# Two transformer blocks: queries scaled by a negative factor when they leave PSUM, a row minimum as the shift of the softmax, and the low parts of the woven-in weights made in two halves

## The chip, the cores and the metric

The kernel runs on one core of one Trainium2 chip. The metric is the time of one execution on the device, in microseconds; the time before is the median of three runs.

## The reference

Two blocks are computed on a sequence of 512 positions with 1024 features, in float32: the first with two layers, the second with one. What matters here are the four softmax attentions. Cut to that:

```python
scale = MLA_QK ** -0.5                          # mla: 8 heads, all 512 keys
s = (einsum('bqhd,bkhd->bhqk', qn, k_nope) + einsum('bqhr,bkr->bhqk', qr, k_r)) * scale
probs = softmax(s, axis=-1)
...
# gqa: 8 heads of 64, a window of 128 keys to either side, alibi slopes 2 ** (-(h + 1)), a sink logit a head
# dsa: 8 heads of 64, the 128 keys that an index score picks, causal by chunks, scale 64 ** -0.5
# mem: 4 heads of 128 over 256 memory rows, scale 128 ** -0.5
```

Around them stand projections, gates, a Fourier mix, a linear recurrence and gated feed-forward networks, all with weights that come from HBM in float32.

## The kernel before, in words

**Products in three parts.** A float32 product with a weight is made of three matmuls: high part by high part, high by low, low by high (`mac`, L549 to L551 for 512 columns). The weights come in one long stream of units of 16 blocks of 128x128 (2048 columns, 1 MB). Every unit goes the same way: SyncE loads it into `raw`, ScalarE (ACT) copies it to `w_hi`, VectorE (DVE) subtracts to get `w_lo` (`split_unit`, L1504) and signals `lo_ready`, which frees both TensorE (PE) to use it and SyncE to load the next but one unit into the same buffer. There are two buffers of each kind.

**The stages.** A layer of the first block has among others z1 and uq (query and key projections), mla, gqa, am, cm, wout, gu and dn; the second block has z2, dsa, mq, mem, mo and again a feed-forward network. The order on each engine is written out by hand; engines meet at semaphores alone.

**Attention.** `attention` exists once for each engine. An item is one head with one block of 128 queries: 32 items in mla, gqa and dsa, 16 in mem, so 176 in the whole program (mla and gqa run twice). For item t

- PE makes the scores (L679) into one of two banks. In gqa and dsa scores are made in pairs, t even and t + 1, once `shift_ready` says that both items before have their shift; in mla and mem one at a time, once the exponential of item t - 2 is done. Behind that it turns the probabilities of item t - 3 (L701), multiplies values (L726, L737), and then does a few blocks of another stage that is woven in: 2 blocks of z1b an item in mla, 3 of am in gqa, 2 of mk in dsa (and mv), none in mem.
- DVE adds the bias where there is one (L1708), takes the row maximum `st_max` (L1713), multiplies it by -scale to `st_neg` (L1714) and signals `shift_ready`; then, for item t - 1, it takes the reciprocal of the sum (L1723) and multiplies the probabilities by it (L1725). Behind that comes `also(t)`: the evictions of the woven-in stage and its split.
- ACT copies the turned probabilities of item t - 3 out of PSUM (`pT`, L1201), and takes the exponential with `st_neg` as bias and the scale as factor (L1212).

**The woven-in stage.** On DVE it is `after_blocks` (L1682): in item t it evicts what PE finished in item t - 1, and splits a unit whose last block PE did in item t - 2.

```python
for b in beside(st, t - 2, per) if t >= 2 else ():
    if b % BLK == BLK - 1 or b == TILES[st][-1][-1]:
        split_unit(c, st, b // BLK)
```

A unit has 16 blocks. Per layer 2 units end in z1b and 6 in am; in the second block 2 end in mk. That makes 18 splits. The two units of mv are split by a call of their own.

**Queries.** They leave PSUM as they are: in z1 and z1b (`qc`) and z2 (`qd`) by `copy_out` (L1533), in uq (`q_a`) by a copy on ACT and a product with the rotary factors on DVE (L1863), in mq (`mq`) by a product with the norm's factor (L2093).

## Time and profile before

| what | value |
|---|---|
| median of 3 runs | 2875.31 us (2872.71 to 2878.05) |
| the profiled execution | 2874.89 us |
| its span | 2873.0 us |
| PE busy | 2727.7 us, 95% |
| DVE busy | 1452.4 us, 51% |
| ACT busy | 1112.2 us, 39% |
| POOL (GpSimd) busy | 378.7 us, 13% |
| granted clock of TensorE, mean | 0.983 of full speed |
| mla, first and second layer, roughly | 211 to 297 us, 1143 to 1227 us |
| gqa, first and second layer, roughly | 297 to 400 us, 1227 to 1338 us |
| dsa, mem, roughly | 2204 to 2293 us, 2434 to 2463 us |

Times in the trace count from the start of the span. PEld is PE's loading of weights, which overlaps its matmuls; L12 is line 12 of the kernel. A row of the timeline gives start, duration, engine, line, operation, and in brackets how long the engine sat idle before it and what released it. Matmuls overlap in their records, so that the sum of durations says little; the distance of starts is what counts.

### The profile page before, as it was taken

To read this page: it belongs to the slowest core of one execution; us is meant where nothing else is said; L and a number is where in the kernel's file an instruction comes from. 1 tells how busy PE (TensorE), PEld (TensorE's weight loads), DVE (VectorE), ACT (ScalarE), POOL (GpSimd) and SP (SyncE) were. 2 spreads that over 40 slices of the span, in tenths; PEclk is the share of its full clock that TensorE was granted. 3 is DMA by queue.
4 is the path that set the end of the run, shared out by engine and by line. 5 is a ranking of instruction groups with operands and counts; after the bars stand their busy time and mean duration, and the time that the engine had idled before them with its cause. 6 is when DMAs were issued, how large, how long until landed. Compare 5 with 4: busy or idle time off the path is not lost. (4 is left out here: it accounts for less than half of the span.)

```text
span 2873.0 us, 37336 instructions
## 1 busy us (share of the span) xinstructions
PE 2727.7 (95%) x13556; PEld 2193.9 (76%) x13556; DVE 1452.4 (51%) x2215; ACT 1112.2 (39%) x1733; POOL 378.7 (13%) x299
## 2 busy tenths in 40 slices
PE   5999999999999799999999999989898899899998
PEld 4876678988887687667898888767686588788886
DVE  5556654533324655665353332455588636634333
ACT  4345543422224434554342222433633534522221
POOL 1010001311102201000131110320011012311101
PEclk9999999999999899999999999999999999999999
DMA  3321122222232232011322223212232122122222
GB/s 125 128 88 45 33 72 96 81 102 96 94 117 88 69 121 99 30 45 60 106 76 96 102 95 111 88 64 83 74 118 74 59 84 93 40 92 88 102 103 88
DMA packets 37057, 245.96 MB, mean 86 GB/s; under 512 B 4144, under 2 KB 5168, under 8 KB 7984
## 3 DMA queue, kind: packets, MB, share of 16 engines
q1 hardware_dynamic: 33600, 239.09, 23.9%
q10 hardware_dynamic: 3312, 4.93, 0.5%
q8 instruction: 91, 1.49, 0.2%
q14 instruction: 54, 0.44, 0.0%
HBM read 241.91 MB, written 2.10 MB: 85 GB/s over the span
## 5 line engine op out<-in xcount | busy, mean ns | idle before, releaser
L549 PE MATMUL bank<-h_hi,w_hi 128*128 128x512 f32 x2024 | 806.4, 398 | 12.1 <-POOL h_lo L2110 4.7
L551 PE MATMUL bank<-h_hi,w_lo 128*128 128x512 f32 x2024 | 791.1, 391 | 0.0
L550 PE MATMUL bank<-h_lo,w_hi 128*128 128x512 f32 x2024 | 791.0, 391 | 0.0
L1504 DVE TENSOR_TENSOR w_lo<-raw,w_hi 128x2048 fp32r<-128x2048 f32 x153 | 353.4, 2310 | 367.1 <-ACT w_hi L1048 365.7
L549 PEld LDWEIGHTS bank<-h_hi,w_hi 128*128 128x128 f32 x2024 | 381.6, 189 | 105.7 <-issue 19.0
L551 PEld LDWEIGHTS bank<-h_hi,w_lo 128*128 128x128 f32 x2024 | 381.4, 188 | 80.8
L550 PEld LDWEIGHTS bank<-h_lo,w_hi 128*128 128x128 f32 x2024 | 381.9, 189 | 79.7 <-issue 3.4
L1048 ACT ACTIVATE w_hi<-raw 128x2048 fp32r<-128x2048 f32 x153 | 291.9, 1910 | 224.1 <-PE bank L551 217.5
L1516 DVE TENSOR_TENSOR w_lo<-raw,w_hi 128x2048 fp32r<-128x2048 f32 x62 | 142.0, 2292 | 158.0 <-ACT w_hi L1260 156.5
L550 PE MATMUL bank<-a_lo,w_hi 128*128 128x512 f32 x528 | 205.4, 389 | 0.0
L549 PE MATMUL bank<-a_hi,w_hi 128*128 128x512 f32 x528 | 205.4, 389 | 0.0
L551 PE MATMUL bank<-a_hi,w_lo 128*128 128x512 f32 x528 | 205.4, 389 | 0.0
L2128 POOL TENSOR_TENSOR a_lo<-res,a_hi 128x512 f32 x66 | 91.3, 1386 | 619.4 <-ACT a_hi L1256 564.1
L1765 DVE TENSOR_TENSOR res<-bank,rstd 128x512 f32<-128x512 f32 x60 | 41.5, 691 | 235.0 <-PE bank L551 235.0
L1256 ACT ACTIVATE a_hi<-res 128x512 f32 x60 | 37.9, 632 | 293.6 <-DVE res L1768 293.6
L1201 ACT ACTIVATE pT<-bank 128x512 f32<-128x512 f32 (+3 forms) x168 | 82.9, 493 | 113.7 <-PE bank L701 112.1
L2110 POOL TENSOR_TENSOR m_lo<-res,m_hi 128x512 fp32r<-128x512 f32 x24 | 31.1, 1294 | 697.0 <-ACT m_hi L1097 697.0
L549 PEld LDWEIGHTS bank<-a_hi,w_hi 128*128 128x128 f32 x528 | 99.1, 188 | 20.8
L551 PEld LDWEIGHTS bank<-a_hi,w_lo 128*128 128x128 f32 x528 | 99.1, 188 | 20.6
L550 PEld LDWEIGHTS bank<-a_lo,w_hi 128*128 128x128 f32 x528 | 99.1, 188 | 20.4
L1260 ACT ACTIVATE w_hi<-raw 128x2048 fp32r<-128x2048 f32 x60 | 114.1, 1902 | 0.0
L1254 ACT ACTIVATE sg<-sg 128x512 f32<-128x512 f32 x60 | 38.0, 633 | 177.3 <-DVE sg L1762 177.3
(397 smaller groups left out, 4401.0 us busy)
## 6 DMA issues: line engine op xcount, KB each, us to landing
raw<-in_stream SPq DMA_DIRECT2D x226, 1024.0 KB, 4.8
x<-in_xT SPq DMA_DIRECT2D x2, 1024.0 KB, 12.6
out_T<-x ACTq DMA_DIRECT2D x8, 256.0 KB, 2.1
p_f<-in_pT ACTq DMA_DIRECT2D x2, 512.0 KB, 3.9
memf<-in_memT ACTq DMA_DIRECT2D x1, 1024.0 KB, 5.6
cst_sb<-in_cst ACTq DMA_DIRECT2D x1, 411.5 KB, 6.5
pos_i<-in_pos ACTq DMA_DIRECT2D x1, 258.0 KB, 9.1
vec<-in_vec ACTq DMA_DIRECT2D x2, 26.0 KB, 1.7
```

The source lines that it names most:

```text
L549: nc.tensor.matmul(ps, wh, xh, start=start, stop=False)
L550: nc.tensor.matmul(ps, wh, xl, start=False, stop=False)
L551: return nc.tensor.matmul(ps, wl, xh, start=False, stop=stop)
L1048: nc.scalar.activation(home(c, v)[0][:, :], raw[v % 2][:, :], ACT.Copy).then_inc(hi_ready, 1)
L1201: nc.scalar.activation(a["pT"][h % 2][:, 0:n, b * P:(b + 1) * P], TURNED[:, 0:n * P].rearrange("p (t q) -> p t q", t=n), ACT.Copy).then_in ...
L1254: nc.scalar.activation(sg[:, p, :], sg[:, p, :], ACT.Silu).then_inc(act_took, 1)
L1256: nc.scalar.activation(a_hi[:, bass.ds(i * 2 + p, 1), :].rearrange("p a s -> p (a s)"), res[:, p, :], ACT.Copy).then_inc(res_hi, 1)
L1260: nc.scalar.activation(w_hi[v][:, :], raw[v][:, :], ACT.Copy).then_inc(hi_ready, 1)
L1504: nc.vector.tensor_tensor(lo[:, :], raw[v % 2][:, :], hi[:, :].bitcast(F32), ALU.subtract).then_inc(lo_ready, 1)
L1516: nc.vector.tensor_tensor(w_lo[s][:, :], raw[s][:, :], w_hi[s][:, :].bitcast(F32), ALU.subtract).then_inc(lo_ready, 1)
L1765: nc.vector.tensor_tensor(res[:, p, :], bank[(t0 + 2 * p + 1) % 4][:, :], rstd[:, 0, :], ALU.mult).then_inc(tile_free, 1)
L2128: nc.gpsimd.tensor_tensor(a_lo[:, bass.ds(i * 2 + p, 1), :].rearrange("p a s -> p (a s)"), res[:, p, :], a_hi[:, bass.ds(i * 2 + p, 1), :] ...
```

## The change

All four attentions now hold negated, scaled logits in PSUM. The queries are multiplied by -scale on their way out of PSUM (`scale_out` in z1, z1b and z2; a factor on ACT and in a three-operand product in uq and mq). The bias gets the opposite sign and loses its factor, the sink as well. The row minimum of that is the shift as it stands, so DVE writes it straight to `st_neg`, and `st_max` and the multiply behind it are gone. The exponential has the factor -1.

The splits of the woven-in stages are cut in two pieces of 1024 columns. The first is made where the whole was made, the second one item later, and the second one signals `lo_ready`. `also` is called once more behind the last item, for the second piece of the last unit. The splits of all other stages, the two of mv among them, stay whole.

```diff
--- before.py
+++ after.py
@@ -260,7 +260,6 @@
         sq = sb("sq", 108, [2, S])
         rstd = sb("rstd", 112, [2, S])
         sq_acc = rstd[:, 1, :]
-        st_max = sb("st_max", 116, [32])
         st_neg = sb("st_neg", 116.25, [32])
         st_sum = sb("st_sum", 116.5, [32])
         st_rec = sb("st_rec", 116.75, [32])
@@ -1185,7 +1184,7 @@
 
                 def set_sink(t):
                     nc.scalar.activation(a["prob"][t % 4][:, 0:1], vv("sink", items[t][0]), ACT.Copy,
-                                         scale=1 / a["scale"]).then_inc(sink_set, 1)
+                                         scale=-1.0).then_inc(sink_set, 1)
                 for t in range(4) if sink else ():
                     set_sink(t)
                 for t in range(len(items) + LAG):
@@ -1210,7 +1209,7 @@
                         n += a.get("first", 0)
                         src = a["prob"][t % 4] if a["biased"] else SCORES[t % 2]
                         nc.scalar.activation(a["prob"][t % 4][:, 0:n], src[:, 0:n], ACT.Exp, bias=st_neg[:, t:t + 1],
-                                             scale=a["scale"], accum_out=st_sum[:, t:t + 1]).then_inc(exp_done, 1)
+                                             scale=-1.0, accum_out=st_sum[:, t:t + 1]).then_inc(exp_done, 1)
                         if sink and t + 4 < len(items):
                             act.wait_ge(exp_done, c.at("I", st, t + 1))
                             set_sink(t + 4)
@@ -1320,7 +1319,7 @@
 
                 def evac_uq(n):
                     if n < 8:
-                        take_hi(c, "uq", n, n, q_a[0:NOPE, n, :], src=lambda ps: ps[0:NOPE, :])
+                        take_hi(c, "uq", n, n, q_a[0:NOPE, n, :], src=lambda ps: ps[0:NOPE, :], scale=-ATT["mla"]["scale"])
                     elif n < 12:
                         j = 2 * (n - 8)
                         take_hi(c, "uq", n, n, k_a[j // 4][0:NOPE, j % 4, :], src=lambda ps: ps[0:NOPE, :])
@@ -1531,6 +1530,10 @@
                 else:
                     dve.wait_ge(tile_done, c.at("T", st, n + 1))
                 nc.vector.tensor_copy(dst, src(ps_of(c, st, n))).then_inc(tile_free, 1)
+
+            def scale_out(c, st, n, dst, factor):
+                dve.wait_ge(tile_done, c.at("T", st, n + 1))
+                nc.vector.tensor_scalar(dst, ps_of(c, st, n)[:, :], factor, None, ALU.mult).then_inc(tile_free, 1)
 
             def pass_on(c, st, n):
 
@@ -1685,9 +1688,19 @@
                     for n, tile in enumerate(TILES[st]):
                         if tile[-1] == b:
                             evac(n)
-                for b in beside(st, t - 2, per) if t >= 2 else ():
-                    if b % BLK == BLK - 1 or b == TILES[st][-1][-1]:
-                        split_unit(c, st, b // BLK)
+                for piece in range(2):
+                    for b in beside(st, t - 2 - piece, per) if t >= 2 + piece else ():
+                        if b % BLK == BLK - 1 or b == TILES[st][-1][-1]:
+                            split_piece(c, st, b // BLK, piece)
+
+            def split_piece(c, st, u, piece):
+
+                v = c.base[st]["U"] + u + 2
+                dve.wait_ge(hi_ready, c.at("U", st, u + 3))
+                at = slice(piece * UC // 2, (piece + 1) * UC // 2)
+                ins = nc.vector.tensor_tensor(w_lo[v % 2][:, at], raw[v % 2][:, at], w_hi[v % 2][:, at].bitcast(F32), ALU.subtract)
+                if piece == 1:
+                    ins.then_inc(lo_ready, 1)
 
             def attention(c, st, bias=None, sink=False, also=None):
                 a = ATT[st]
@@ -1710,8 +1723,7 @@
                             n += lo
                         if sink:
                             dve.wait_ge(sink_set, c.layer * len(items) + (t + 1))
-                        link(nc.vector.reduce_max(st_max[:, t:t + 1], src[:, 0:n], AX_X))
-                        nc.vector.tensor_scalar(st_neg[:, t:t + 1], st_max[:, t:t + 1], -a["scale"], None, ALU.mult).then_inc(shift_ready, 1)
+                        nc.vector.tensor_reduce(st_neg[:, t:t + 1], src[:, 0:n], AX_X, ALU.min).then_inc(shift_ready, 1)
                     if a["per_tile"] == 2 and t % 8 == 3 and 11 <= t < len(items):
                         output_lo(c, st, taken)
                         taken += 1
@@ -1728,6 +1740,8 @@
                             taken += 1
                     if also is not None:
                         also(t)
+                if also is not None:
+                    also(len(items) + 2)
                 while taken < a["heads"] // a["per_tile"]:
                     output_lo(c, st, taken)
                     taken += 1
@@ -1854,13 +1868,14 @@
                             nc.vector.scalar_tensor_tensor(out=dst, in0=cq[:, j, :], scalar=vv("q_norm", j) if j < 3 else vv("kv_norm"),
                                                            in1=rstd[:, j // 3, :], op0=ALU.mult, op1=ALU.mult).then_inc(res_ready, 1)
                     else:
-                        copy_out(c, "z1", n, n, qc[:, n - 6, :], lambda ps: ps[:, :], wait_act=False)
+                        scale_out(c, "z1", n, qc[:, n - 6, :], -ATT["gqa"]["scale"])
                 stage_loop(c, "z1", evac_z1)
 
                 def evac_uq(n):
                     if n < 8:
                         dve.wait_ge(act_took, c.at("A", "uq", n + 1))
-                        nc.vector.tensor_tensor(q_a[64:P, n, :], ps_of(c, "uq", n)[64:P, :], cs[64:P, :], ALU.mult).then_inc(tile_free, 1)
+                        nc.vector.scalar_tensor_tensor(out=q_a[64:P, n, :], in0=ps_of(c, "uq", n)[64:P, :], scalar=-ATT["mla"]["scale"],
+                                                       in1=cs[64:P, :], op0=ALU.mult, op1=ALU.mult).then_inc(tile_free, 1)
                     elif n < 12:
                         j = 2 * (n - 8) + 1
                         copy_out(c, "uq", n, n, k_a[j // 4][0:NOPE, j % 4, :], lambda ps: ps[64:P, :])
@@ -1874,7 +1889,7 @@
                     link(nc.vector.tensor_tensor(dist[:, b, 0:n], dist[:, b, 0:n], cst_sb[:, CST["window"] + off:CST["window"] + off + n], ALU.add))
                 def evac_z1b(n):
                     if n < 2:
-                        copy_out(c, "z1b", n, 0, qc[:, 2 + n, :], lambda ps: ps[:, :], wait_act=False)
+                        scale_out(c, "z1b", n, qc[:, 2 + n, :], -ATT["gqa"]["scale"])
                     else:
                         dve.wait_ge(act_took, c.at("A", "z1b", 1))
                         pass_on(c, "z1b", 2)
@@ -1883,7 +1898,7 @@
 
                 def alibi(h, b):
 
-                    return dist[:, b, 0:len(windowed(b)) * P], -(2.0 ** (-8.0 * (h + 1) / HEADS)) * HD ** 0.5
+                    return dist[:, b, 0:len(windowed(b)) * P], 2.0 ** (-8.0 * (h + 1) / HEADS)
                 def add_am(n):
 
                     if n % 2 == 1:
@@ -2020,7 +2035,10 @@
                         link(nc.vector.tensor_scalar(wsc[:, :, :], vw[:, :, HD:HD + 8], 8 ** -0.5, None, ALU.mult))
                 else:
                     dst = {8: ki, 22: kk}.get(n)
-                    copy_out(c, "z2", n, 0, qd[:, n - 18, :] if dst is None else dst[:, :], lambda ps: ps[:, :], wait_act=False)
+                    if dst is None:
+                        scale_out(c, "z2", n, qd[:, n - 18, :], -ATT["dsa"]["scale"])
+                    else:
+                        copy_out(c, "z2", n, 0, dst[:, :], lambda ps: ps[:, :], wait_act=False)
                 for t in idx_items(n):
                     add_idx(t)
                 if n >= 18:
@@ -2082,7 +2100,7 @@
                     left("mv", (t - 28) // 4, (t - 28) // 4)
                 if t in (25, 33):
                     split_unit(c, "mv", (t - 25) // 8)
-            attention(c, "dsa", lambda h, b: (score[:, b, 0:(b + 1) * P], 1.0), also=evac_mem)
+            attention(c, "dsa", lambda h, b: (score[:, b, 0:(b + 1) * P], -1.0), also=evac_mem)
             merge(c, 2, "cm", 2)
             project_norm(c, "wout", "post1", 2, "mix_post", "normh")
             for half in range(2):
@@ -2090,8 +2108,9 @@
                 for p in range(2):
                     dve.wait_ge(tile_done, c.at("T", "mq", 2 * half + p + 1))
                     for g in range(2):
-                        ins = nc.vector.tensor_tensor(mq[:, 2 * p + g, cols(half)], ps_of(c, "mq", 2 * half + p)[:, cols(g)],
-                                                      rstd[:, 0, cols(half)], ALU.mult)
+                        ins = nc.vector.scalar_tensor_tensor(out=mq[:, 2 * p + g, cols(half)], in0=ps_of(c, "mq", 2 * half + p)[:, cols(g)],
+                                                             scalar=-ATT["mem"]["scale"], in1=rstd[:, 0, cols(half)],
+                                                             op0=ALU.mult, op1=ALU.mult)
                     ins.then_inc(tile_free, 1)
                 if half == 0:
                     for u in range(2):
```

**Where instructions move.** Both places are on DVE. The first is gqa, items 12 to 13, where a unit of am is split; `prob_1_120` before and `prob_1_119` now are the probabilities of item 13, and `prob_0` are those of item 12. Before:

```order
L1497 REGISTER_ALU
L1504 TENSOR_TENSOR w_lo_53<-raw_49,w_hi_51 128x2048
L1700 REGISTER_ALU
L1708 SCALAR_TENSOR_TENSOR prob_1_120<-dist,bank 128x384
L1490 REGISTER_ALU
L1712 REGISTER_ALU
L1713 TENSOR_REDUCE st_max<-prob_1_120 128x1
L1490 REGISTER_ALU
L1714 TENSOR_SCALAR st_neg<-st_max 128x1
L1723 RECIPROCAL st_rec<-st_sum 128x1
L1490 REGISTER_ALU
L1725 TENSOR_SCALAR prob_0_119<-prob_0_119,st_rec 128x384
```

Now:

```order
L1699 REGISTER_ALU
L1701 TENSOR_TENSOR w_lo_53<-raw_49,w_hi_51 128x1024
L1713 REGISTER_ALU
L1721 SCALAR_TENSOR_TENSOR prob_1_119<-dist,bank 128x384
L1489 REGISTER_ALU
L1725 REGISTER_ALU
L1726 TENSOR_REDUCE st_neg<-prob_1_119 128x1
L1735 RECIPROCAL st_rec<-st_sum 128x1
L1489 REGISTER_ALU
L1737 TENSOR_SCALAR prob_0_118<-prob_0_118,st_rec 128x384
L1701 TENSOR_TENSOR w_lo_53<-raw_49,w_hi_51 128x1024
```

Before the whole split stands ahead of item 13's bias, reduce and negation; now one half stands there and the other behind the product of item 12's probabilities, and the negation is gone.

The second is mem, two items in the middle of the stage, where nothing is woven in. Before:

```order
L1713 TENSOR_REDUCE st_max<-bank 128x1
L1714 TENSOR_SCALAR st_neg<-st_max 128x1
L1723 RECIPROCAL st_rec<-st_sum 128x1
L1725 TENSOR_SCALAR prob_m_174<-prob_m_174,st_rec 128x256
L1713 TENSOR_REDUCE st_max<-bank 128x1
L1714 TENSOR_SCALAR st_neg<-st_max 128x1
L1723 RECIPROCAL st_rec<-st_sum 128x1
L1725 TENSOR_SCALAR prob_m_175<-prob_m_175,st_rec 128x256
```

Now:

```order
L1726 TENSOR_REDUCE st_neg<-bank 128x1
L1735 RECIPROCAL st_rec<-st_sum 128x1
L1737 TENSOR_SCALAR prob_m_173<-prob_m_173,st_rec 128x256
L1726 TENSOR_REDUCE st_neg<-bank 128x1
L1735 RECIPROCAL st_rec<-st_sum 128x1
L1737 TENSOR_SCALAR prob_m_174<-prob_m_174,st_rec 128x256
```

Four instructions an item have become three, and the reduce writes `st_neg` itself.

## Rows read from the trace of the kernel before

**Rows 1.** The page, part 1: busy us (share of the span) xinstructions

```profile
PE 2727.7 (95%) x13556; PEld 2193.9 (76%) x13556; DVE 1452.4 (51%) x2215; ACT 1112.2 (39%) x1733; POOL 378.7 (13%) x299
```

**Rows 2.** Stretches: length, PE, PEld, DVE, ACT, POOL busy (x), PEclk, DMA, GB/s

```profile
211.00:297.00 86.00, 80.12 (x524) 51.92 (x524) 56.22 (x141) 50.55 (x109) 0.00 (x0) 1.00 0.11 38
297.00:400.00 103.00, 98.66 (x551) 70.06 (x552) 72.94 (x182) 53.52 (x140) 0.00 (x0) 1.00 0.15 52
2204.00:2293.00 89.00, 69.32 (x446) 45.90 (x448) 66.61 (x174) 48.11 (x116) 6.32 (x6) 0.88 0.15 49
2434.00:2463.00 29.00, 22.45 (x81) 11.91 (x81) 17.59 (x69) 16.63 (x51) 0.00 (x0) 0.94 0.00 1
```

**Rows 3.** Waits of PE, whole span, then dsa: us in total, times, longest

```profile
PE bank L679 <- DVE st_neg L1714: 19.3, 15, 3.4
PE bank L679 <- DVE st_neg L1714: 13.5, 11, 3.4
```

**Rows 4.** Timeline, one item of dsa: start us, us, engine, line, operation

```profile
2223.75 0.69 DVE L1713 TENSOR_REDUCE st_max<-prob 128x1 f32<-128x512 f32 x1
2224.47 0.15 DVE L1714 TENSOR_SCALAR st_neg<-st_max 128x1 f32<-128x1 f32 x1
2224.54 0.15 DVE L1723 RECIPROCAL st_rec<-st_sum 128x1 f32<-128x1 f32 x1
```

**Rows 5.** Timeline, dsa: a short wait of PE; in brackets idle before, releaser

```profile
2274.44 0.92 PE L679 MATMUL bank<-kk,qd 64*128 64x384 f32 x4 [0.21 <-DVE st_neg L1714]
```

**Rows 6.** Timeline, mem: two items

```profile
2441.52 0.70 PE L679 MATMUL bank<-mk,mq 128*128 128x256 f32 x2
2442.47 0.38 ACT L1201 ACTIVATE pT<-bank 128x256 f32<-128x256 f32 x1
2442.90 0.48 ACT L1212 ACTIVATE prob_m<-bank,st_neg 128x256 f32<-128x256 f32 x1
2443.52 0.70 PE L679 MATMUL bank<-mk,mq 128*128 128x256 f32 x2
```

**Rows 7.** Timeline, mla of layer 1: its start, and behind the last split

```profile
219.26 1.12 PE L679 MATMUL bank<-k_a,q_a 128*128 128x512 f32 x2 [2.89 <-ACT prob L1212]
259.67 0.30 PEld L679 LDWEIGHTS bank<-k_a,q_a 128*128 128x128 f32 x2 [0.42 <-ACT prob L1212]
```

**Rows 8.** Groups of DVE by form: xcount, busy us, mean ns, idle before

```profile
L1504 DVE TENSOR_TENSOR w_lo<-raw,w_hi 128x2048 fp32r<-128x2048 f32 x153 | 353.4, 2310 | 367.1 <-ACT w_hi L1048 365.7
L1714 DVE TENSOR_SCALAR st_neg<-st_max 128x1 f32<-128x1 f32 x176 | 27.0, 154 | 6.0
L1533 DVE COPY qc<-bank 128x512 f32<-128x512 f32 x8 | 5.5, 686 | 0.9 <-PE bank L551 0.9
L1500 DVE TENSOR_TENSOR w_lo<-raw,w_hi 128x1024 fp32r<-128x1024 f32 x2 | 2.5, 1225 | 2.7 <-ACT wm_hi L1046 2.7
```

**Rows 9.** Timeline, gqa of layer 1: items 12 to 16

```profile
339.13 2.29 DVE L1504 TENSOR_TENSOR w_lo<-raw,w_hi 128x2048 fp32r<-128x2048 f32 x1
342.01 0.55 DVE L1713 TENSOR_REDUCE st_max<-prob 128x1 f32<-128x385 f32 x1
342.59 0.15 DVE L1714 TENSOR_SCALAR st_neg<-st_max 128x1 f32<-128x1 f32 x1
342.80 0.70 PE L679 MATMUL bank<-kdup,qc 64*128 64x256 f32 x4 [1.46 <-DVE st_neg L1714]
346.12 0.15 DVE L1714 TENSOR_SCALAR st_neg<-st_max 128x1 f32<-128x1 f32 x1
349.38 0.70 PE L679 MATMUL bank<-kdup,qc 64*128 64x256 f32 x4
```

**Rows 10.** The page, part 6: raw's DMA, KB each, us to landing

```profile
raw<-in_stream SPq DMA_DIRECT2D x226, 1024.0 KB, 4.8
```

**Rows 11.** Stretches with half the clock (column PEclk), dsa and mla of layer 2

```profile
2242.00:2244.00 2.00, 2.00 (x7) 0.50 (x5) 0.38 (x1) 0.20 (x2) 0.00 (x0) 0.50 0.00 0
1150.00:1152.00 2.00, 2.00 (x5) 1.19 (x5) 0.46 (x1) 0.68 (x2) 0.00 (x0) 0.50 0.00 0
```

## The prediction

> **What bounds the kernel now.** I read the page first. TensorE (PE) is busy for 95% of the span and VectorE (DVE) for 51% [rows 1], so work taken off DVE is worth nothing where PE is fed. What matters is where PE waits for DVE, and the stretches by stage show it [rows 2]: PE is idle for 5.9 us of 86 in the first attention of a layer (mla), 4.3 of 103 in the second (gqa), 19.7 of 89 in dsa and 6.5 of 29 in mem. The second layer repeats mla and gqa, with the same waits. All idle time of PE in attention is thus some 47 us, and much of it is at the stages' ends, for reasons that the change does not touch.
>
> Next I read who releases PE. Over the whole span it waits 15 times, 19.3 us in all, for the negation st_neg (L1714), before a pair of score products (L679); 11 of these waits, 13.5 us, lie in dsa, and the other four, 5.8 us, in gqa, two a layer [rows 3]. In mem and mla, whose scores wait for the exponential, the same negation stands one step further back. So the four stages have to be priced one by one.
>
> **The negation goes.** Per item DVE now runs reduce, negation, reciprocal, product. In dsa the reduce starts at 2223.75 and lasts 0.69, the negation starts at 2224.47, the reciprocal at 2224.54 [rows 4]. Two savings have to be kept apart. *Latency*: what waits for the shift is released at the reduce's end (2224.44) and not at the negation's (2224.62): 0.18 us. *Pace*: the reciprocal starts 0.08 before the negation ends; if it does the same behind the reduce it starts at 2224.36 in place of 2224.54, which is 0.18 too. All 176 negations at 0.18 are 32 us of DVE time; that is no forecast, only the ceiling.
>
> Here a rule bears on the pace. The Trainium skill (VectorE: DVE Perf Modes, "The DRAIN you can't avoid") has the next instruction start only when the pipeline has emptied, though a later section lets one that is not held start earlier. By the first rule the reciprocal could not start before 2224.44, the pace would gain 0.10, and the sum below would be about 10 us in place of 11.5. The rows show overlap in this very place, and I follow them.
>
> *dsa.* Scores come in pairs, and a pair waits until both items before it have their shift. Where it waits, one item gives its pace and the other its latency, 0.36 together. Eleven waits by 0.36 are 4.0 us. Two of them are short, as the one shown (0.21) [rows 5], so I take off 0.1 for these. The two pairs that hold a mk split pay for two halves, 0.15 each more (below), and get nothing back, because both halves fall into the same pair of items: off with 0.3. Rounded, **3.5 us**. Bounds: 0, if another releaser stands right behind; 4.0 and the lapse of the clock below.
>
> *mem.* Items follow each other every 1.0 us, and the loop holds two: a score product at 2441.52, its reduce and negation, its exponential at 2442.90, and the next score product but one at 2443.52, right behind the exponential. Yet ACT is busy with the copy pT until 2442.85 [rows 6]. Between 0.05 (nothing overlaps) and 0.18 can be won a double step; I take 0.13, as ACT too starts an instruction a little before the end of the one ahead. With four double steps that is 0.5, and 0.18 each at the start, behind the first row of values and at the end: **1.0 us** (bounds 0 and 1.5).
>
> *mla.* At its start PE waits 2.89 for the first exponential, which comes 0.18 earlier; afterwards PE is fed until the last z1b unit is split after item 13. There w_lo holds up the reduce of item 14, its exponential comes late, and the weight load of the score product at 259.67 waits 0.42 for it [rows 7]. With the half in place of the whole the shift comes more than 1 us earlier, but PE is free only 0.42 earlier. 0.18 and 0.42 are 0.6 a layer; with a trifle at the end **1.3 us** for both (bounds 0 and 2.5, twice the 1.25 that the half and the negation take off the shift).
>
> **The low parts by halves.** A whole w_lo takes 2.310 us on average, 2.29 in the stage; the two halves of the same size that four1 has already take 1.225 each [rows 8, 9]. A unit therefore costs 0.15 more, 18 units 2.8 us of DVE time in all, hidden beside PE except in the two dsa pairs above. What is won is only where the halves fall on two sides of a pair. In gqa a unit ends with items 5, 10, 15, 21, 26 and 31, its split comes two items later, behind 7, 12, 17, 23, 28 and 33. Behind an odd item both halves fall into the next pair, and nothing changes; PE does not wait there now. Behind 12 and 28 the first half stays in the pair and the second goes to the next. These are exactly the two waits of gqa: w_lo at 339.13, the reduce at 342.01, the negation at 342.59, and PE at 342.80 after 1.46 us of waiting [rows 9]. The half takes 1.07 off (2.29 less 1.22), the negations of items 12 and 13 take 0.36: 1.43 of 1.46. The wait vanishes, and nothing is behind it: PE waits there for the shift alone. The second half then runs in the next pair, which has no am tile to merge and no output to take: there the second item's negation came at 346.12, and PE wanted it at 349.38 [rows 9]. Four waits by 1.43: **5.7 us** (bounds 0 and 6.1).
>
> What is late next: lo_ready is signalled by the second half, one item (some 3 us) later. A unit's low part is done three to four items before PE's first use of it, so two to three remain. The same signal lets SP fetch the next unit; it lands 4.8 us later in the median [rows 10] and ACT wants it about ten items on. At the end of gqa both halves follow each other behind the last item, 0.15 longer, with 8 blocks of PE work ahead of their first reader. ACT's order is unchanged, and neither POOL nor SP gets or loses an instruction.
>
> **The scale at the eviction.** Twelve copies of query tiles become a multiply by a constant. A copy from PSUM takes 0.686 [rows 8]; I take the same, as the source is what is common. In mla's q_a and mem's mq a product gets a constant as a third factor. All lie behind ACT or beside PE, but for the last two mq products ahead of mem's first score: between 0 and +0.1, taken as 0. Sink, bias factor and the exponential's scale are other constants in the same instructions.
>
> **Sum.** 5.7 + 3.5 + 1.0 + 1.3 = 11.5 us. The profiled execution took 2874.9 us (its span of 2873.0 and 1.9 around it), so 2863.4; the median of the three runs is 0.4 above this execution: **2863.8**.
>
> **The rivals.** A difference under 0.2%, 5.8 us, is about what a measurement of this kernel cannot tell from none.
>
> *The halves buy nothing.* If the second half meets the next pair with too little room, the gqa waits move by two items and only the negations count: 4 x 0.36 there, 3.5 in dsa, 1.0 in mem, little in mla: about 6, or less with the lower pace, so 2869 to 2871. For it: DVE is busy 71% of gqa. Against it: in the pair that follows, 3 us are to spare. Chance 0.17, most of it inside 0.2%.
>
> *The clock stays up as well.* The granted clock was 0.50, PE's 1.2 GHz level, at 2242 in dsa and at 1150 in the second layer's mla [rows 11], each time right behind a wait of PE; behind the other waits for the shift it kept its level. In 2 us at the half clock PE does the work of 1; each lapse lasts somewhat longer, so both cost some 2.5 us. If shorter waits keep the clock, these are won too: 2861.3. The Trainium skill (TensorE: Matmul & The Clock Gate, on oscillation) likewise ties the fall to idle gaps. But the waits only shrink by 0.2 to 0.4, and a fall may as well come elsewhere. Chance 0.15.
>
> *The minimum is slower than the maximum.* The reduce is the one instruction that all 176 items keep in another form. Were it to take two steps an element, a 512-wide one would last 1.22, like a half with its 1024 elements, and not 0.69. dsa would then lose 0.34 - 0.18 an item (5 us), mem 3 us, mla's loop through the exponential 0.35 a pair (7 us), against 2.6 still won in gqa: 12 us slower, 2887. It decides from 0.18 us more an item on, where the saving is eaten up. No row of the trace has a minimum by a reduce; against it speaks that a copy (0.686) and a maximum (0.69) of 512 elements take the same [rows 4, 8], so that the operation seems not to matter. Chance 0.03.
>
> **How the numbers follow.** The forecast itself has 0.65; it spans 2859 to 2868 by the bounds above. The range takes in the clock and the upper part of the first rival: 2857 to 2870. Faster by over 0.2% needs under 2869.6: 0.65 + 0.15 + 0.04 of the first rival = 0.84. Within 0.2%: 0.13. Slower: 0.03.
>
> **What would show it.** Right: no wait of PE for the shift in gqa; the eleven in dsa each about 0.36 shorter, the sum near 9.5; mem's step at 0.94; L1714's group gone, a reduce st_neg of 0.69, w_lo halves of 1.22. Wrong: a wait of PE for the shift two items later in gqa; a wait for lo_ready; a minimum that takes longer than 0.69; a reciprocal that starts no earlier behind the reduce than it did.

## The result, and the profile after

| | median us | runs |
|---|---|---|
| before, on the same chip | 2875.39 | 4, 2872.71 to 2878.05 |
| the changed kernel | 2853.48 | 4, 2850.28 to 2855.95 |

The ratio is 0.9923, 95% interval 0.9906 to 0.9940: 21.9 us faster. The forecast was 2863.8 with a range of 2857 to 2870, so the sign was right and the size was not; the time is below the range. Three more comparisons of the same pair, further down, gave -12.5, -18.5 and -18.8 us.

The page of the changed kernel, part 1, beside [rows 1]. Its line numbers have moved: L679 is now L678, L1713 and L1714 are L1726, L1723 is L1735, L1504 is L1503; L1701 is new, the halves.

```profile
PE 2720.9 (95%) x13556; PEld 2189.7 (77%) x13556; DVE 1429.2 (50%) x2057; ACT 1111.6 (39%) x1733; POOL 379.0 (13%) x299
```

DVE has 158 instructions fewer: 176 negations gone, 18 halves more. The stretches that answer to [rows 2] (length, PE, PEld, DVE, ACT, POOL busy, PEclk, DMA, GB/s), for mla and gqa of the first layer, dsa and mem:

```profile
210.80:297.00 86.20, 81.28 (x524) 52.51 (x523) 51.57 (x110) 49.48 (x108) 0.00 (x0) 0.98 0.11 38
297.00:397.50 100.50, 99.03 (x556) 70.26 (x554) 67.96 (x155) 53.96 (x140) 0.00 (x0) 1.00 0.14 45
2193.00:2276.80 83.80, 68.55 (x448) 45.74 (x448) 61.98 (x144) 48.69 (x116) 6.54 (x7) 0.91 0.15 51
2417.70:2444.00 26.30, 20.96 (x79) 11.25 (x80) 15.69 (x53) 15.47 (x51) 0.00 (x0) 1.00 0.00 1
```

By these windows gqa is 2.5 us shorter, dsa 5.2, mem 2.7. The waits of PE for the shift over the whole span, against [rows 3]:

```profile
PE bank L678 <- DVE st_neg L1726: 9.7, 8, 3.0
```

All eight are in dsa, which had eleven; the four of gqa are gone. Three waits of dsa in the kernel before, and behind them the same three after, by the timeline:

```profile
2221.87 1.13 PE L679 MATMUL bank<-kk,qd 64*128 64x512 f32 x4 [1.54 <-DVE st_neg L1714]
2226.71 0.49 PE L679 MATMUL bank<-kk,qd 64*128 64x128 f32 x4 [0.76 <-DVE st_neg L1714]
2241.51 2.08 PE L679 MATMUL bank<-kk,qd 64*128 64x512 f32 x4 [2.12 <-DVE st_neg L1714]
```

```profile
2209.36 1.13 PE L678 MATMUL bank<-kk,qd 64*128 64x512 f32 x4 [1.17 <-DVE st_neg L1726]
2213.83 0.49 PE L678 MATMUL bank<-kk,qd 64*128 64x128 f32 x4 [0.39 <-DVE st_neg L1726]
2227.95 1.13 PE L678 MATMUL bank<-kk,qd 64*128 64x512 f32 x4 [1.75 <-DVE st_neg L1726]
```

Each is 0.37 shorter: latency and pace, as forecast. The third row shows something more. Before, the same four matmuls took 2.08 us behind their wait; now they take 1.13. That is the clock, the term that the forecast missed, though this row alone does not show a gain: this profile has another lapse (a stretch at half clock) at 2246, behind a wait where the kernel before has none, and in two of the four profiles of the changed kernel a lapse still starts 1.1 and 1.5 us behind this same wait (2230.3 in after_third, 2234.8 in after_again).

dsa's largest lapse begins ahead of every wait that the change shortens. In the kernel before the clock stands at half from 2203.9 to 2217.6, and it falls during the stage's first wait, which is for another result and keeps its 5.8 us in the changed kernel:

```profile
2205.08 0.80 PE L679 MATMUL bank<-kk,qd 64*128 64x128 f32 x4 [5.76 <-DVE rstd L1671]
2212.14 1.23 PE L679 MATMUL bank<-kk,qd 64*128 64x256 f32 x4 [3.40 <-DVE st_neg L1714]
```

gqa of the first layer, items 12 to 16, against [rows 9]:

```profile
339.10 1.23 DVE L1701 TENSOR_TENSOR w_lo<-raw,w_hi 128x1024 fp32r<-128x1024 f32 x1
340.91 0.55 DVE L1726 TENSOR_REDUCE st_neg<-prob 128x1 f32<-128x385 f32 x1
341.52 0.30 PEld L678 LDWEIGHTS bank<-kdup,qc 64*128 64x128 f32 x4 [0.44 <-DVE st_neg L1726]
341.52 0.70 PE L678 MATMUL bank<-kdup,qc 64*128 64x256 f32 x4
341.91 1.22 DVE L1701 TENSOR_TENSOR w_lo<-raw,w_hi 128x1024 fp32r<-128x1024 f32 x1
344.98 0.42 DVE L1726 TENSOR_REDUCE st_neg<-prob_gqa 128x1 f32<-128x257 f32 x1
348.11 0.30 PEld L678 LDWEIGHTS bank<-kdup,qc 64*128 64x128 f32 x4 [0.35 <-issue]
348.11 0.70 PE L678 MATMUL bank<-kdup,qc 64*128 64x256 f32 x4
```

The first half alone stands ahead of the reduce. An idle 0.44 remains ahead of the load of weights, where the next pair, which waits for nothing, has 0.35 by issue; the matmuls themselves show none. The second half runs in the next pair, whose last shift is ready at 345.40 and wanted at 348.11: nothing is late.

The groups of DVE by form, against [rows 4, 8]:

```profile
L1726 DVE TENSOR_REDUCE st_neg<-bank 128x1 f32<-128x512 f32 x64 | 44.0, 690 | 40.8 <-PE bank L678 37.8 <-DVEq L1541 2.3
L1701 DVE TENSOR_TENSOR w_lo<-raw,w_hi 128x1024 fp32r<-128x1024 f32 x36 | 43.8, 1222 | 8.3 <-ACT w_hi L1047 7.7
L1536 DVE TENSOR_SCALAR qc<-bank 128x512 f32<-128x512 f32 x8 | 5.5, 687 | 0.9 <-PE bank L550 0.8
```

The minimum costs what the maximum did, a half 1.22, a scaled copy what a copy did (686).

**Code and clock apart.** I lined up PE's instructions of two traces one by one and read how their distance grows over each stage; where the granted clock was below 1, I added up the length of the stretch times (1 - PEclk), in steps of 2 us, and call that the *clock lost*. The rest of a stage's difference is *code*. Clock is lost in portions: nearly every lapse loses 1.7 us or a multiple of it. Clock lost is an upper bound of what a lapse costs, since matmuls at half speed cost nothing where PE would have waited anyway; 5.1 of the 49.5 us even lie behind PE's last matmul, which ends at 2858.9, while the clock falls at 2863 for the rest of the span. The profiled executions differ by 18.9 us in span: 10.6 are code, 8.3 clock (49.5 us lost before, 41.2 after).

### The profile page after: what moved, and what is told of

It reads as the page before. It is cut to its first block and busy times, and to the rows that moved or that the text cites. A ratio compares the mean times of both kernels' runs of the same rounds, so it can differ in the third digit from the quotient of the medians.

```text
span 2854.1 us, 37054 instructions
## 1 busy us (share of the span) xinstructions
PE 2720.9 (95%) x13556; PEld 2189.7 (77%) x13556; DVE 1429.2 (50%) x2057; ACT 1111.6 (39%) x1733; POOL 379.0 (13%) x299
## 5 line engine op out<-in xcount | busy, mean ns | idle before, releaser
L1503 DVE TENSOR_TENSOR w_lo<-raw,w_hi 128x2048 fp32r<-128x2048 f32 x135 | 312.2, 2314 | 361.2 <-ACT w_hi L1047 360.6
L1515 DVE TENSOR_TENSOR w_lo<-raw,w_hi 128x2048 fp32r<-128x2048 f32 x62 | 142.0, 2292 | 158.0 <-ACT w_hi L1259 156.5
L550 PEld LDWEIGHTS bank<-a_hi,w_lo 128*128 128x128 f32 x528 | 99.1, 188 | 20.4
```

Source lines behind the costliest of these rows:

```text
L550: return nc.tensor.matmul(ps, wl, xh, start=False, stop=stop)
L1503: nc.vector.tensor_tensor(lo[:, :], raw[v % 2][:, :], hi[:, :].bitcast(F32), ALU.subtract).then_inc(lo_ready, 1)
L1515: nc.vector.tensor_tensor(w_lo[s][:, :], raw[s][:, :], w_hi[s][:, :].bitcast(F32), ALU.subtract).then_inc(lo_ready, 1)
```

## The experiments

There were fourteen further runs of nine kernels, on four chips, each beside runs of the kernel before on the same chip. Clock and clock lost are means over all executions, those of the result included (its runs of the kernel before, for which no clocks are listed, are left out):

| kernel | runs | median us, each time | against before | mean clock | clock lost, us | span x clock, us |
|---|---|---|---|---|---|---|
| before | 85 | 2872.1, 2875.2, 2874.7, 2876.0 | | 0.9826 | 50.1 +-0.4 | 2822.0 |
| changed | 20 | 2853.5, 2859.5, 2856.7, 2855.9 | -21.9, -12.5, -18.5, -18.8 | 0.9853 | 41.8 +-0.9 | 2812.8 |
| neg_only | 10 | 2862.1, 2860.0 | -10.0, -14.7 | 0.9852 | 42.3 +-1.0 | 2816.8 |
| halves_only | 11 | 2867.4 | -4.6 | 0.9839 | 46.1 +-0.9 | 2819.1 |
| neg_twice | 6 | 2887.9 | +12.7 | 0.9818 | 52.4 +-1.4 | 2832.3 |
| fill_dsa | 11 | 2873.4 | -1.3 | 0.9833 | 48.0 +-0.4 | 2823.4 |
| pair_first | 10 | 2846.4, 2846.8 | -28.8, -27.9 | 0.9855 | 41.3 +-1.0 | 2804.1 |
| whole_mk | 5 | 2855.6 | -20.4 | 0.9852 | 42.3 +-1.7 | 2812.5 |
| pair_whole_mk | 4 | 2846.1 | -29.9 | 0.9868 | 37.7 +-0.7 | 2806.5 |

Clock lost is here the span times (1 - clock) of each run, with the standard error of the mean; one execution scatters by 3 to 4 us in most kernels. Span x clock is roughly the time at full clock throughout. The row of the kernel before puts four chips together, and they differ: it lost 48.4 us on one (32 executions) and 51.0, 51.0 and 51.7 on the others, so that a difference to a kernel that ran on one chip is better taken there. From the profiles, the code per stage against the trace of before, in us:

| profile | mla | gqa | dsa | mem | clock lost in dsa |
|---|---|---|---|---|---|
| before; before_again, before_third | 0; -0.1, -0.2 | 0; 0, +0.1 | 0; -0.5, -0.7 | 0; 0, -0.9 | 11.9; 10.2, 13.7 |
| changed, four profiles | -0.9 to -1.0 | -5.7 | -3.8, -4.0, -4.7, -3.9 | -0.9 | 10.2, 11.9, 10.2, 10.3 |
| neg_only, two | -0.8, -0.9 | -1.5 | -2.2, -2.2 | -0.9 | 5.1, 5.1 |
| halves_only | 0.0 | -4.2 | -0.5 | 0.0 | 13.6 |
| neg_twice | +4.0 | +1.6 | +1.7 | -0.4 | 15.4 |
| fill_dsa | -0.1 | 0.0 | +3.5 | -1.5 | 6.8 |
| pair_first, two | -0.9 | -5.7 | -11.1, -11.1 | -0.9 | 6.8, 6.8 |
| whole_mk | -0.9 | -5.8 | -4.9 | -0.9 | 10.2 |
| pair_whole_mk | -1.0 | -5.7 | -10.0 | -0.9 | 6.8 |

Where is the clock lost? In the four attentions and a few us around them the three profiles of the kernel before lose 17.1, 17.1 and 22.2 us, the four of the changed kernel 11.9, 17.1, 15.4 and 11.9, the two of neg_only 10.2 and 10.2. Everywhere else it is 29 to 34, 29 to 33, and 27 and 31 us. In the mean 4.7 us of the changed kernel's gain in these profiles lie in the attentions, where the waits changed, and 1.8 elsewhere, where nothing did.

### The kernel before, unaltered

Two theories stood against each other. A: the changed kernel has fewer lapses because PE waits less. B: the difference in clock was luck of those runs. A2, further down, is A with a number of lapses that varies from run to run.

> The kernel before, unchanged, once more, for the time and the granted clock of several runs and a second trace. In the first pair of traces 8.3 us of the 18.9 us between the profiled executions are stretches of half clock (49.5 against 41.2 us of lost clock), each such stretch costing about 1.7 us. Theory A (the clock belongs to the kernel: fewer and shorter waits of TensorE let it fall less often): mean clock 0.983 again within 0.001 in every run, so 2872 to 2878 us. Theory B (the clock was luck of those runs): clocks from 0.983 to 0.988 and times from 2860 to 2878, with time minus lost clock the same, about 2826, in all of them.

> The kernel before as a submission of its own, unaltered, as the measure of what the clock does with no change in the program. Both theories expect the time of the shared runs of the kernel before within 1 us. Theory B allows its mean clock to differ from theirs by as much as the kernels' clocks differ from each other (0.001 or more); Theory A expects it within 0.0005 of them.

2872.43 us (ratio 1.000, 0.9991 to 1.0009) and 2874.62 us (0.9995, 0.9986 to 1.0005). The same program's profiles show 49.5, 51.1 and 51.2 us of clock lost, in mostly the same places, and their mean clocks (0.9829 and 0.9824) are within 0.0004 of those of the other runs of the kernel before on the same chips. Luck moves a single execution by 4 us or so; the mean over ten or twenty moves by about 1, and from chip to chip by up to 3. Theory A's 0.983 within 0.001 in every run was too narrow (0.982 to 0.986 on that chip), but nothing came near theory B's 0.988 and 2860 us. The -0.9 of mem in before_third is no gain: there a lapse fell on matmuls ahead of a wait, and its loss is overstated.

### One part alone

neg_only has the scale at the eviction and the minimum, and whole splits; halves_only the halves, with their call behind the last item, and maximum, negation and scales as before. First the core of neg_only, then of halves_only:

```diff
-                        link(nc.vector.reduce_max(st_max[:, t:t + 1], src[:, 0:n], AX_X))
-                        nc.vector.tensor_scalar(st_neg[:, t:t + 1], st_max[:, t:t + 1], -a["scale"], None, ALU.mult).then_inc(shift_ready, 1)
+                        nc.vector.tensor_reduce(st_neg[:, t:t + 1], src[:, 0:n], AX_X, ALU.min).then_inc(shift_ready, 1)
```

```diff
-                for b in beside(st, t - 2, per) if t >= 2 else ():
...
-                        split_unit(c, st, b // BLK)
+                for piece in range(2):
+                    for b in beside(st, t - 2 - piece, per) if t >= 2 + piece else ():
...
+                            split_piece(c, st, b // BLK, piece)
```

> The change with whole splits: negation gone, minimum, scaled queries. Work and waits by the stages of the first two traces: dsa 3.8, mem 1.0, gqa 4 x 0.36 = 1.4, mla 0.3, so 6.5 us at an equal clock. Theory A: the clock recovers for the part of the waits that dsa and mem lose, 0.985, some 5 us more: 2863. Theory B: 2869 at a clock of 0.983, or any clock between 0.983 and 0.988 regardless of the kernel.

> The kernel before with the woven-in splits by halves, the negation kept. At an equal clock: gqa 4 x 1.07 = 4.3, mla 0.2, less 0.3 in dsa: 4.2 us. The waits of gqa shrink to 0.4 and stay. Theory A: clock 0.984 to 0.985, some 2 to 4 us more: 2867. Theory B: 2871 at 0.983. If the two parts need each other (the wait in gqa vanishes only with both), neg_only and halves_only together give less than the whole change.

> The changed kernel once more. Theory A: clock 0.986 to 0.988 again, 2850 to 2856 us, and the stretches of half clock lie at other places than in the first trace in part, since only their number belongs to the kernel. Theory B: clocks as spread as those of before_again, 2850 to 2866 us.

neg_only: 2862.11 us, ratio 0.9966 (0.9952 to 0.9979). halves_only: 2867.45, 0.9982 (0.9973 to 0.9991). Both together, the changed kernel again: 2859.54, 0.9952 (0.9938 to 0.9965). Waits of PE for the shift over the whole span, neg_only and then halves_only:

```profile
PE bank L678 <- DVE st_neg L1716: 14.3, 12, 3.0
```

```profile
PE bank L679 <- DVE st_neg L1724: 15.0, 14, 3.4
```

Within dsa they are 9.9 us in 8 and 13.4 in 10. So in gqa neg_only keeps four waits of 1.10 (1.46 less 0.36), halves_only four of 0.40 (1.46 less 1.07): exactly the two terms of the forecast, and with both the wait is gone. The code of gqa adds up too, -1.5 and -4.2 against -5.7. In dsa and mem the negation earns the gain, the halves next to nothing. At full clock (last column of the first table) neg_only is worth 5.2 and halves_only 2.9; the changed kernel, with both, is worth 9.2.

In these runs the changed kernel gained little clock (0.9840 against 0.9833), and its 2859.5 us lie outside theory A's 2850 to 2856; neg_only (0.9848, 2862.1) came out as theory A had it. Luck of the runs, theory B, was still open.

### The changed kernel again, and a second dose

```diff
                         link(nc.vector.reduce_max(st_max[:, t:t + 1], src[:, 0:n], AX_X))
+                        link(nc.vector.tensor_scalar(st_max[:, t:t + 1], st_max[:, t:t + 1], 1.0, None, ALU.mult))
```

> The changed kernel once more, unaltered. Two comparisons of it have given -21.9 us and -12.5 us against the kernel before, and the sum of its waits and instructions, read from the traces, is some 10.6 us in both. Theory A (the lower share of half-clock stretches belongs to the changed kernel): the runs show a mean granted clock at least 0.002 above those of the kernel before, and a time 16 to 20 us shorter. Theory B (what the clock gives is luck of the runs or of the session): a difference of clock of either sign under 0.001 and a time 9 to 13 us shorter. In both the product of time and clock is 10 to 11 us below that of the kernel before.

> The kernel before, with one more small multiply of the maximum ahead of the negation of each item of the attentions, a second dose of what the change takes away. The theory of the waits: the product of time and clock grows by about what neg_only took off, 6 us (limits 4 to 9), since the same waits of gqa and dsa and the step of mem get longer by one more small instruction of 0.15 to 0.18 us. Theory A on the clock (longer waits of TensorE make more half-clock stretches): the mean clock falls by another 0.001 to 0.0015 below the kernel before, and the time grows by 9 to 11 us. Theory B (luck): the clock is that of the kernel before within 0.0005, and the time grows by 5 to 7 us.

> The changed kernel unaltered, in a fourth comparison. Three have given -21.9, -12.5 and -18.5 us, and mean clocks of 0.9868, 0.9840 and 0.9852 where the kernel before had 0.9832 and 0.9821 in the last two. Theory A2 (the changed kernel has on average fewer half-clock stretches, since TensorE waits less, and their number varies from run to run): a mean clock 0.001 to 0.003 above that of the kernel before, a time 13 to 20 us shorter, and a product of time and clock 10 to 11 us shorter. Theory B (luck of runs and sessions): a clock difference of either sign, and times 9 to 13 us shorter.

> The negation taken out alone, once more. It gave 0.9848 of clock against 0.9832, and 6.1 us of the product of time and clock. Theory A2: again a clock 0.0005 to 0.002 above that of the kernel before, and a time 8 to 12 us shorter. Theory B: the clock of the kernel before within 0.0005, and a time 5 to 7 us shorter.

after_third: 2856.71 us, ratio 0.9937 (0.9923 to 0.9950), clock 0.9852 against 0.9821. after_fourth: 2855.86, 0.9933 (0.9920 to 0.9947), 0.9858 against 0.9823. neg_only_again: 2859.99, 0.9950 (0.9936 to 0.9963), 0.9856 against 0.9823. Theory B forecast 9 to 13 us for the changed kernel and 5 to 7 for neg_only, and falls with 18.5, 18.8 and 14.7; the last is also more than the 8 to 12 that theory A2 allowed. Over all runs the changed kernel loses 8.3 +-1.0 us of clock less than the kernel before, neg_only 7.8 +-1.1. Taken chip by chip it is 2.6, 8.7 and 10.4 us for the changed kernel and, on the first and third of these chips, 4.9 and 9.8 for neg_only: the sign is the same each time, the size is known less well than the +-1.0 says. halves_only ran on the first of these chips alone and lost 2.2 +-1.1 less there (4.0 against the mean of all chips). That the clock goes with the program is shown; that it goes by the shorter waits is what the next runs try.

neg_twice: 2887.88 us, ratio 1.0039 (1.0024 to 1.0054), +12.7; at full clock +10.3, over the limit of 9. Its waits for the shift:

```profile
PE bank L679 <- DVE st_neg L1715: 22.9, 14, 3.8
```

They grew by 3.6 us (15.6 in dsa, 7.3 in gqa: four of 1.83, which is 1.46 and 0.36 more). What I had not reckoned with is mla: PE's instructions fall back by 2.0 us a layer, in the second layer by 0.2 at its start and by 0.5 to 0.7 at each of three places (1186 to 1191, 1200 to 1203, 1215 to 1219 in the trace before), in steps of 0.17 to 0.37 ahead of scores and transposes. My reading is that the kernel before ran mla just inside the loop through the exponential, and that one more small instruction an item puts PE outside; no run tried it. A dose more thus costs four times in mla what a dose less saves (4.0 against 0.9). The clock was 0.9818, 0.0003 to 0.0006 lower than before where theory A had 0.0010 or more: by its own numbers it missed here, and the relation between waiting and clock is not a straight line.

### Do the idle times make the lapses?

fill_dsa gives PE more work where it waits, and takes away nothing: each transpose of the probabilities in dsa is done twice, the second over the first.

```diff
-                        for j in range(n):
+                        for j in [j for j in range(n) for _ in range(2 if st == "dsa" else 1)]:
```

> The kernel before with each of the 80 transposes of the probabilities in dsa done twice, the second over the first: TensorE gets some 8.8 us more of matmuls (0.11 us each in a train) in a stage in which it waits 13.5 us for the shift. It tells whether it is the idle time of TensorE that makes the half-clock stretches. Theory A2: the clock lost in dsa, 10.2 to 13.7 us in the three profiles of the kernel before, falls to 5 to 9 us, and the mean clock of the run rises by 0.001 to 0.002; the work costs 1 to 5 us at full clock, since most of it lies where TensorE waits, so that the time changes by -4 to +3 us. Theory B, or another cause than idleness: the clock lost in dsa stays at 10 to 14 us, and the time grows by 1 to 6 us.

2873.43 us, ratio 0.9994 (0.9985 to 1.0003). 100 us with dsa in them, of the kernel before and then of fill_dsa:

```profile
2200.00:2300.00 100.00, 76.32 (x472) 51.30 (x473) 70.45 (x181) 50.66 (x121) 8.23 (x8) 0.88 0.16 53
```

```profile
2200.00:2300.00 100.00, 81.59 (x556) 58.29 (x555) 72.37 (x186) 50.92 (x121) 8.21 (x8) 0.93 0.17 57
```

The waits of PE for the shift in dsa, in fill_dsa:

```profile
PE bank L679 <- DVE st_neg L1714: 10.2, 8, 3.4
```

PE is busy 5.3 us longer, the waits for the shift in dsa fell from 13.5 us in 11 to 10.2 in 8, and the clock lost there from 10.2 to 13.7 (three profiles) to 6.8 (one). The stage's code takes 3.5 us more. So 80 matmuls that compute nothing new were paid for by the clock: theory A2 holds in dsa, as far as one profile tells. The rival that is left is that any change of what PE does in dsa shifts the lapses; one profile cannot tell the two apart. Over the whole run the clock lost is 2.1 us less (48.0 against 50.1), or 2.9 +-1.1 against the runs on the same chip, at the lower end of what was expected, since in this profile 6.8 us were lost from mem on, where the kernel before lost 1.7 to 5.1.

A second place shows the same without any added work. In gqa of the second layer the last wait for the shift (1.5 us) comes some 10 us ahead of the stage's end (PE starts at 1326.39), and the kernel before falls at that end. Four stretches of it, and the same place in the changed kernel:

```profile
1334.00:1336.00 2.00, 1.22 (x14) 0.84 (x14) 0.83 (x2) 1.98 (x2) 0.00 (x0) 1.00 0.00 0
1336.00:1338.00 2.00, 1.40 (x10) 0.92 (x10) 2.00 (x1) 0.38 (x1) 0.00 (x0) 0.73 0.00 0
1338.00:1340.00 2.00, 2.00 (x7) 1.56 (x6) 0.73 (x2) 1.81 (x2) 0.00 (x0) 0.50 0.49 90
1340.00:1342.00 2.00, 2.00 (x10) 1.61 (x9) 0.00 (x0) 0.07 (x1) 0.00 (x0) 0.91 0.84 356
```

```profile
1324.00:1326.00 2.00, 1.98 (x11) 1.40 (x9) 0.50 (x2) 0.16 (x1) 0.00 (x0) 1.00 0.47 193
1326.00:1328.00 2.00, 1.22 (x14) 0.84 (x14) 1.15 (x2) 1.98 (x2) 0.00 (x0) 1.00 0.00 0
1328.00:1330.00 2.00, 0.80 (x10) 0.59 (x10) 1.66 (x2) 0.97 (x3) 0.00 (x0) 1.00 0.00 0
```

PE is no less idle right there, but the 1.5 us of waiting ahead of it are gone, and the clock stays at 1.00. All seven profiles of kernels with whole splits in gqa have this lapse; of the nine with halves one has it (after_again). So these 1.7 us belong to the halves.

### The order by pairs

If PE waits for both shifts of a pair, VectorE should do both before anything else. pair_first is the changed kernel with that order in dsa: bias and minimum of items t and t + 1, then reciprocal and product of the items before them, and the woven-in work.

```diff
-                for t in range(len(items) + 2):
-                    if t < len(items):
+                def front(t):
+                    if t < len(items):
...
+                def back(t):
...
+                steps = [[t] for t in range(len(items) + 2)]
+                if st == "dsa":
+                    steps = [[t, t + 1] for t in range(0, len(items) + 2, 2)]
+                for step in steps:
+                    for t in step:
+                        front(t)
+                    for t in step:
+                        back(t)
```

> The changed kernel, with VectorE in dsa doing the bias and the minimum of both items of a pair before the reciprocal and the product of either. TensorE waits for the shift of the second item before the next pair of score matmuls, and ahead of that shift VectorE now does the reciprocal and product of the item before (0.15 and 0.42 to 0.49 us). If these lie in the way, as the order of the instructions says: each of the 8 waits left in dsa (9.7 us in all) gets shorter by 0.4 to 0.6 us, and the time falls by 3 to 5 us against the changed kernel. Rival: in dsa VectorE is busy 62 of 84 us and the products only come later, so that TensorE waits for the probabilities at its transposes what it saved at the scores, and the time stays within 1 us of the changed kernel's, or gets longer by up to 3 us.

> The order by pairs in dsa once more, in another session. It gave 2846.4 against 2856.7 us of the changed kernel, 7.1 us of the product of time and clock and a clock of 0.9860 against 0.9852. Theory A2: 8 to 12 us below the changed kernel, with a clock at least as high. Theory B: 6 to 8 us below it in the mean, with a clock difference of either sign.

2846.43 us, ratio to the kernel before 0.9902 (0.9888 to 0.9917), and 2846.75, 0.9907 (0.9893 to 0.9921): 10.3 and 9.1 us below the changed kernel on the same chip (2845.47 to 2848.30 against 2855.48 to 2857.34 in the first, without overlap). The timeline of one pair:

```profile
2228.11 0.69 DVE L1726 TENSOR_REDUCE st_neg<-prob 128x1 f32<-128x512 f32 x1
2228.72 0.68 DVE L1721 SCALAR_TENSOR_TENSOR prob<-score,bank 128x512 f32<-128x512 f32 x1
2229.43 0.69 DVE L1726 TENSOR_REDUCE st_neg<-prob 128x1 f32<-128x512 f32 x1
2230.03 0.15 DVE L1738 RECIPROCAL st_rec<-st_sum 128x1 f32<-128x1 f32 x1
2230.24 0.49 PE L678 MATMUL bank<-kk,qd 64*128 64x128 f32 x4
```

and PE's waits for the shift in dsa:

```profile
PE bank L678 <- DVE st_neg L1726: 3.4, 2, 3.0
```

6.3 of 9.7 us are gone, and 3.0 of the rest is the stage's first pair, which has nothing ahead of it. The gain at full clock is 8.7, not 3 to 5: I had counted the reciprocal and product between the two reduces, and left out what else stood there. In the changed kernel's timeline of VectorE, one item to the next:

```profile
2224.93 0.55 DVE L1726 TENSOR_REDUCE st_neg<-prob 128x1 f32<-128x384 f32 x1
2225.40 0.15 DVE L1735 RECIPROCAL st_rec<-st_sum 128x1 f32<-128x1 f32 x1
2225.59 0.35 DVE L1737 TENSOR_SCALAR prob<-prob,st_rec 128x256 f32<-128x256 f32 x1
2226.75 0.56 DVE L1721 SCALAR_TENSOR_TENSOR prob<-score,bank 128x384 f32<-128x384 f32 x1 [0.81 <-DVEq L1541]
```

Behind the product VectorE waits 0.81 us to pass on a tile of mk that ScalarE evicts (L1541); elsewhere a split or the low part of an output lies there. That all of this has moved behind both minima is in the order of the program; what each is worth was not tried by itself. The rival, that the transposes would wait instead, fell: dsa's code is 7 us shorter than the changed kernel's in both profiles. The clock is only 0.5 us better in the mean, though lapses in dsa went from 10 to 12 us lost to 6.8; in pair_first_again it was even lower than the changed kernel's on the same chip (0.9850 against 0.9858), against theory A2.

### Why the two parts' clock does not add

> The changed kernel with the low parts of dsa (the weights of the memory keys) in one piece again, and the halves kept beside mla and gqa. In dsa the profiles of neg_only lose 5.1 us of clock, both times, those of the changed kernel 10.2 to 11.9, the ones of the kernel before 10.2 to 13.7. Theory D (the halves in dsa bring back the falls that the missing negation had ended there): the lost clock in dsa is 5.1 us again, the code of dsa takes 1 to 2 us more than in the changed kernel, and the time is 2 to 5 us below the changed kernel's 2856. Rival (the pattern of falls in dsa hangs on where the stage begins, or on luck, not on the halves): 8 to 12 us lost in dsa, and a time 0 to 3 us above 2856.

> The order by pairs in dsa with the low parts of dsa in one piece again. Theory D: the lost clock of dsa, 6.8 us in both profiles of the order by pairs, falls to 5.1 us or less, the code takes up to 2 us more, and the time is within 2 us of 2847. Rival: 6.8 us or more are lost in dsa, and the time is 0 to 4 us above 2847, since VectorE stands in the way for 2.3 us at a time.

```diff
-                for piece in range(2):
+                for piece in range(1 if st == "mk" else 2):
...
+                            if st == "mk":
+                                split_unit(c, st, b // BLK)
+                            else:
+                                split_piece(c, st, b // BLK, piece)
```

whole_mk: 2855.59 us, ratio 0.9931 (0.9917 to 0.9945), 10.2 us lost in dsa. pair_whole_mk: 2846.11, 0.9893 (0.9878 to 0.9908), 6.8 lost. Theory D falls twice: the halves in dsa do not bring the lapses back. In code they are worth nothing there in the changed kernel (-4.9 without them, -3.8 to -4.7 with them) and 1.1 us in the order by pairs (-10.0 against -11.1), where the waits for the shift are 4.2 us in 4 without them and 3.4 in 2 with them. Why neg_only loses 5.1 us in dsa, the changed kernel 10.2 or more, with the same waits in the stage (9.9 and 9.7 us in 8), stays open: what differs lies ahead of dsa, in when it is reached or in what PE did before. With 0.9893 pair_whole_mk has the lowest ratio of all, but it is within a microsecond of pair_first.

## Why the prediction was wrong

The terms of the sum, each against its measurement (code of the four profiles of the changed kernel; for dsa less the mean of the kernel before's own three profiles, -0.4):

| step | forecast | measured |
|---|---|---|
| gqa | 5.7 | 5.7 |
| dsa | 3.5 | 3.7 (its waits 13.5 to 9.7) |
| mem | 1.0 | 0.9 |
| mla | 1.3 | 0.9 |
| sum | 11.5 | 11.2 |
| clock | 0 in the sum, 2.5 in a rival | 8.3 less lost |

- *Latency and pace, 0.18 each.* Right. In dsa a reduce starts at 2227.34, lasts 0.55 and is followed by the reciprocal at 2227.81, 0.08 before its end. The main rule of the Trainium skill (VectorE: DVE Perf Modes, "The DRAIN you can't avoid") would have had it start at the end; the measurement decides for the overlap, which the same section allows to an instruction that is not held.

```profile
2227.34 0.55 DVE L1726 TENSOR_REDUCE st_neg<-prob 128x1 f32<-128x384 f32 x1
2227.81 0.15 DVE L1735 RECIPROCAL st_rec<-st_sum 128x1 f32<-128x1 f32 x1
```

- *dsa.* Right: its waits stand at 9.7 us where about 9.5 was forecast. Seven of the eight are 0.31 to 0.38 shorter than before. The eighth grew from 0.22 to 0.39, as the lapse ahead of it is gone; of the three that vanished two were short (0.44 and 0.21), and the third (0.77) is covered by the new lapse at 2246.
- *gqa.* Right to the tenth, and nothing came in the wait's place. The first rival (the halves buy nothing) falls: no wait two items later.
- *mem.* Right in sum, not in place: two items take 1.95 (2423.72 to 2425.67) where 1.87 was forecast and 2.00 stood, but the first three steps are 0.19 shorter each.
- *mla.* The wait of 0.42 at the second z1b unit is gone (its load follows 0.17 behind, by issue, so that 0.25 of the 0.42 came back), the start is 0.17 earlier, as forecast. The "trifle at the end" did not come.
- *The scale at the eviction, the minimum.* Right: 687 and 690 ns. The third rival falls.
- *The clock: the step that failed.* The text took it as unchanged in the likeliest case, with the ground that "the waits only shrink by 0.2 to 0.4, and a fall may as well come elsewhere", and priced the rival by two lapses at 2.5 us. The trace of before held some 49 us of clock lost, not just the two lapses [rows 11]; I looked at two, one behind a wait for the shift and one behind a wait for the exponential. Nor is it so that "behind the other waits for the shift it kept its level": behind the longest, 3.40 us up to 2212.14, it stood at half already. What the runs showed in its place: over 20 and 85 runs the changed kernel loses 8.3 us of clock less (2.6, 8.7 and 10.4 on three chips), some five lapses, where the sum had 0 and the rival 2.5; neg_only, which shortens waits by just those 0.36 us, loses 7.8 less.

  The lapse at 2242 is gone in the changed kernel's first profile (the four matmuls that took 2.08 us take 1.13) and in one more of the four, with one at 2246 or 2247 in its place; in the other two a lapse starts 1.1 to 1.5 us behind the same wait; the words "a fall may as well come elsewhere" were right here, and dsa as a whole lost 10 to 12 us still; the one at 1150 is gone in one of four, and one that I had not named, behind gqa of the second layer, in three of four. The Trainium skill's page (TensorE: Matmul & The Clock Gate, on oscillation) ties the fall to idle gaps; fill_dsa and the lapse behind gqa agree, while neg_only and the changed kernel, with 9.9 and 9.7 us of the same waits in dsa and 5.1 and 10.2 us or more lost there, show that the waiting does not give the number. Which waits removed which lapses stays open.

How the sum closes: 17.5 us is the mean difference over all these runs, 11.2 of code leave 6.3 for the clock. That is less than 8.3, as lapses that cover a wait cost less than they lose; by span x clock the parts are 9.2 and 8.3. Between these two ways to divide it stays open. In the first comparison the changed kernel's four runs lost 37.8 us, 4 less than in its mean: about that much of its 21.9 us is luck.

## What to carry to other kernels

Price a change by the wait it shortens, and each wait by what stands ahead of its releaser: that was right to a few tenths here. Then list every stretch below full clock, also those behind stages' ends, and treat the clock as a term with a range of its own, as wide as several lapses: a change that took a few tenths off each wait went with some five lapses fewer in the mean. If a producer works for a consumer that waits for two results at once, let it make both before it does anything else: that order was worth another 9 to 10 us, without an instruction less.

## What the runs showed of the hardware

- A lapse of the granted clock to half loses 1.7 us, several in a row a multiple; a run of this kernel loses some 50 us by them, 5 of them behind PE's last matmul, and the number varies by two or three between executions of one program (granted clock 0.979 to 0.986 for the kernel before, 0.983 to 0.988 for the changed one).
- Places and amounts repeat by program: dsa lost 5.1 and 5.1 us in neg_only, 6.8 in all three profiles of the order by pairs, 10.2 to 11.9 in five of the changed order.
- 80 more matmuls in dsa cost nothing that the runs could tell (2873.4 against 2874.7 us): 3.5 us more of code in dsa, and 3 to 7 us less of clock lost there, in one profile.
- The clock does not scale with the waiting: pair_first waits for the shift 10.9 us less than neg_only (3.4 against 14.3) and loses hardly less clock (41.3 against 42.3; on the chip that ran both 42.7 against 41.2).
